# Gated norm of the state space branch: Silu(z) at its eviction, one product per row, one pair of ones matmuls, the norm's weight in the split

## What is computed

```python
z_ssm, xbc, dt_raw, q, k, v, z_att, f_logit, g_logit = jnp.split(proj, offsets, axis=-1)
y_ssm = _ssd_branch(z_ssm, xbc, dt_raw, ...)
...
def _rmsnorm(x, w):
    y = xf * lax.rsqrt(jnp.mean(xf * xf, axis=-1, keepdims=True) + EPS)
    return (y * w.astype(jnp.float32)).astype(x.dtype)
...
    # end of _ssd_branch
    return _rmsnorm(y * jax.nn.silu(z), ssm_norm_w)
...
merged = g_ssm * jnp.einsum("bse,ed->bsd", y_ssm, w_proj_ssm) + ...
```

## Time and profile before

| what | value |
|---|---|
| timed executions, median | 2098.41 us (2098.94, 2098.41, 2094.1) |
| profiled execution, its own time | 2096.4 us |
| its span in the trace | 2094.9 us |
| what lies around the span | 1.5 us |
| mean granted clock of TensorE | 0.973 of full speed |
| TensorE busy | 1967.2 us (94%) |
| stage 2 in the trace | about 209 to 445 us |
| stage 3 | about 445 to 510 us |
| stage 4 | from 510 us |

### The profile page before, as it was taken

One profiled execution on the slowest core, in us unless ns is written; L12 is line 12 of the kernel. 1 busy time (PEld: TensorE's weight loads), 2 busy tenths in 40 slices (PEclk: granted clock), 3 DMA queues, 4 the chain that ended last, 5 costly groups with the idle time before them and its releaser, 6 DMA issues. The chain is left out here.

```text
span 2094.9 us, 26015 instructions
## 1 busy us (share of the span) xinstructions
PE 1967.2 (94%) x9712; PEld 1580.1 (75%) x9712; DVE 997.0 (48%) x1217; ACT 756.3 (36%) x1136; POOL 167.2 (8%) x311
## 2 busy tenths in 40 slices
PE   6899999998999999999999999879999998999897
PEld 3678778776787887888878788657777776787786
DVE  4576544555422334333343344488333335554865
ACT  4423233234213443444433342242343434422422
POOL 0000110000010000000000000012100002101100
PEclk8899999999999999999999999999999999999999
DMA  7441665533431111111111443423201111111302
GB/s 284 170 72 41 101 112 99 111 111 120 140 103 39 41 40 50 30 40 40 40 50 40 141 131 101 140 58 89 88 21 43 33 30 60 43 48 28 129 28 90
DMA packets 165319, 166.35 MB, mean 79 GB/s; under 512 B 11402, under 2 KB 143938, under 8 KB 163970
## 3 DMA queue, kind: packets, MB, share of 16 engines
q1 hardware_dynamic: 151746, 116.11, 18.0%
q0 software_dynamic: 13504, 49.29, 10.3%
HBM read 132.22 MB, written 33.16 MB: 79 GB/s over the span
## 5 line engine op out<-in xcount | busy, mean ns | idle before, releaser
L288 PE MATMUL acc<-ha_hi,w_hi 128*128 128x512 f32 x1152 | 471.6, 409 | 11.5 <-ACT nxt L301 7.2
L288 PE MATMUL acc<-ha_hi,w_lo 128*128 128x512 f32 x1152 | 453.0, 393 | 0.0
L288 PE MATMUL acc<-ha_lo,w_hi 128*128 128x512 f32 x1152 | 452.1, 392 | 0.0
L288 PEld LDWEIGHTS acc<-ha_hi,w_hi 128*128 128x128 f32 x1152 | 218.7, 190 | 57.4 <-issue 11.6
L288 PEld LDWEIGHTS acc<-ha_hi,w_lo 128*128 128x128 f32 x1152 | 218.0, 189 | 48.4
L288 PEld LDWEIGHTS acc<-ha_lo,w_hi 128*128 128x128 f32 x1152 | 218.9, 190 | 42.1
L257 DVE TENSOR_TENSOR w_lo<-w_raw,w_hi 128x1024 fp32r<-128x1024 f32 x128 | 157.5, 1230 | 140.2 <-ACT w_hi L253 137.2
L271 PE MATMUL acc<-ha_hi,w_hi 128*128 128x512 f32 x592 | 188.0, 399 | 27.9 <-DVE ha_lo L1740 13.7
L271 PE MATMUL acc<-ha_lo,w_hi 128*128 128x512 f32 x592 | 185.0, 394 | 0.0
L271 PE MATMUL acc<-ha_hi,w_lo 128*128 128x512 f32 x592 | 184.8, 394 | 0.0
L271 PEld LDWEIGHTS acc<-ha_hi,w_hi 128*128 128x128 f32 x592 | 111.1, 191 | 58.7 <-issue 15.8
(11 more groups left out here) (437 smaller groups left out, 2777.1 us busy)
## 6 DMA issues: line engine op xcount, KB each, us to landing
w_raw<-in_w_in SPq DMA_DIRECT2D x99, 512.0 KB, 3.9
w_ada<-in_w_ada SPq DMA_DIRECT2D x8, 1024.0 KB, 11.8
acs_bc<-acs_scr POOLq DMA_DIRECT2D x8, 1024.0 KB, 15.9
w_raw<-in_w_out SPq DMA_DIRECT2D x11, 512.0 KB, 3.9
x_tok<-in_x SPq DMA_DIRECT2D x8, 512.0 KB, 6.5
xt_scr<-xt SPq DMA_DIRECT2D x1, 4096.0 KB, 22.6
w_ada_g<-in_w_ada SPq DMA_DIRECT2D x8, 512.0 KB, 9.7
z_scr<-stash SPq DMA_DIRECT2D x8, 512.0 KB, 10.8
```

The lines of the kernel that those rows point to most:

```text
L288: mm = pe.matmul(acc[:, 0, half * HALF:(half + 1) * HALF], w[:, n % 2, k, :], x[:, k, half * HALF:(half + 1) * HALF], start=(k == 0 and i ...
```

## The change

- `read_half` takes a function, and the z tiles of stage 2 are read from PSUM with Silu in place of Copy. z_scr then holds silu(z), and stage 3 has no Silu.
- Stage 3 forms one product per row, xbc = xbc * silu_z. ya_hi is Copy(xbc) with the norm's weight as a scale per partition; ya_lo is xbc * weight - ya_hi in one VectorE operation. Squares go to y_sq, a buffer of two rows, in the place of yw.
- VectorE adds all 8 squared rows into xbc row 0 (7 additions in place of 4), and the ones matmuls read that row alone (2 in place of 8).
- On VectorE the product of row f + 1 stands ahead of the low part of row f. The order of the gate reads and the weight splits on ScalarE and VectorE is another, and the split of tile 31 (N_MIX1) has a place of its own.

```diff
@@ -291,14 +291,14 @@
...
-        def read_half(act, n, half, m, dst, adv=0):
+        def read_half(act, n, half, m, dst, adv=0, func=ACT.Copy):
 
             if half:
                 projected(act, n, adv=adv)
             else:
                 act.wait_ge(half_done, m + 1)
             s = slice(half * HALF, (half + 1) * HALF)
-            return act.activation(dst[:, s], acc[:, 0, s], ACT.Copy).then_inc(fill_free, 1)
+            return act.activation(dst[:, s], acc[:, 0, s], func).then_inc(fill_free, 1)
 
...
@@ -971,7 +971,7 @@
             def read_tile(c, i):
                 act.wait_ge(stash_saved[i], 16 * c + 16)
                 for half in range(2):
-                    read_half(act, N_Z + 2 * c + i, half, 2 * c + i, stash[:, i, :])
+                    read_half(act, N_Z + 2 * c + i, half, 2 * c + i, stash[:, i, :], func=ACT.Copy if i else ACT.Silu)
                 act.drain().then_inc(stash_ready[i], 1)
 
...
@@ -1078,8 +1078,8 @@
         silu_z = Region(at_arena + XBC_TILES * T * 4, arena_end)("silu_z", [P, 2, T])
-        yw = Region(at_arena + 8 * T * 4, arena_end)("yw", [P, 2, T])
-        z_loaded, z_silued = [sem("z_loaded0"), sem("z_loaded1")], sem("z_silued")
+        y_sq = Region(at_arena + 8 * T * 4, arena_end)("y_sq", [P, 2, T])
+        z_loaded, sq_added = [sem("z_loaded0"), sem("z_loaded1")], sem("sq_added")
...
@@ -1121,67 +1121,78 @@
         def act_3(act):
             begin_stage(act, 3)
             act.drain().then_inc(ga_saved, 16)
-            for j in range(2):
-
-                def silu(b):
-                    f = 4 * j + b
-                    act.wait_ge(z_loaded[b % 2], 16 * (f // 2) + 16)
-                    act.activation(silu_z[:, b % 2, :], silu_z[:, b % 2, :], ACT.Silu).then_inc(z_silued, 1)
-
-                def tile(b):
-
-                    act.wait_ge(yz_done, 4 * j + b + 3)
-                    act.activation(xbc[:, 4 * j + b, :], xbc[:, 4 * j + b, :], ACT.Square).then_inc(Norm.squared, 1)
-                    act.activation(ya_hi[:, 4 * j + b, :], yw[:, b % 2, :], ACT.Copy).then_inc(x_hi_done, 1)
-
-                def gate(i, half):
-                    n = N_GATT + 2 * j + i
-                    projected(act, n)
-                    act.wait_ge(ga_saved, 64 * j + 32 * i + 16 * half + 16)
-                    e = act.activation(ga_half[:, :], acc[:, n % 2, half * HALF:(half + 1) * HALF], ACT.Copy)
-                    if half:
-                        e.then_inc(acc_free[n % 2], 1)
-                    act.drain().then_inc(ga_ready, 1)
-
-                if j:
-                    split_hi(act, N_GATT + 3)
-                silu(0)
-                silu(1)
-                tile(0)
-                silu(2)
-                tile(1)
-                gate(0, 0)
-                split_hi(act, N_GATT + 2 + 2 * j)
-                silu(3)
-                tile(2)
-                gate(0, 1)
-                tile(3)
-                gate(1, 0)
-                gate(1, 1)
+
+            def tile(f):
+                act.wait_ge(yz_done, f + 3)
+                act.activation(ya_hi[:, f, :], xbc[:, f, :], ACT.Copy, scale=dcol(vec1, VEC1, "ssm_norm_w", f)).then_inc(x_hi_done, 1)
+                if f >= 2:
+                    act.wait_ge(sq_added, f - 1)
+                act.activation(y_sq[:, f % 2, :], xbc[:, f, :], ACT.Square).then_inc(Norm.squared, 1)
+
+            def gate(i, half):
+                n = N_GATT + i
+                projected(act, n)
+                act.wait_ge(ga_saved, 32 * i + 16 * half + 16)
+                e = act.activation(ga_half[:, :], acc[:, n % 2, half * HALF:(half + 1) * HALF], ACT.Copy)
+                if half:
+                    e.then_inc(acc_free[n % 2], 1)
+                act.drain().then_inc(ga_ready, 1)
+
+            for f in range(3):
+                tile(f)
+            gate(0, 0)
+            split_hi(act, N_GATT + 2)
+            tile(3)
+            gate(0, 1)
+            tile(4)
+            tile(5)
+            gate(1, 0)
+            split_hi(act, N_GATT + 3)
+            tile(6)
+            gate(1, 1)
+            tile(7)
+            gate(2, 0)
+            split_hi(act, N_MIX1)
+            gate(2, 1)
+            gate(3, 0)
             split_hi(act, N_MIX1 + 1)
+            gate(3, 1)
             end_stage(act, 3)
 
         def dve_3(dve):
             begin_stage(dve, 3)
             dve.drain().then_inc(yz_done, 2)
-            for f in range(KT):
-                b = f % 2
-                if f and b == 0:
-                    split_lo(dve, N_GATT + f // 2 + 1)
-                dve.wait_ge(z_silued, f + 1)
-                dve.scalar_tensor_tensor(yw[:, b, :], xbc[:, f, :], dcol(vec1, VEC1, "ssm_norm_w", f), silu_z[:, b, :],
-                                         ALU.mult, ALU.mult)
-                dve.tensor_tensor(xbc[:, f, :], xbc[:, f, :], silu_z[:, b, :], ALU.mult)
+
+            def gated(f):
+                dve.wait_ge(z_loaded[f % 2], 16 * (f // 2) + 16)
+                dve.tensor_tensor(xbc[:, f, :], xbc[:, f, :], silu_z[:, f % 2, :], ALU.mult)
                 dve.drain().then_inc(yz_done, 1)
+
+            def low(f):
                 dve.wait_ge(x_hi_done, SPLITS[3] + f + 1)
                 if f == 6:
                     for i in range(2):
                         dve.wait_ge(stash_saved[i], 16 * (NCHUNK + 1))
-                dve.tensor_tensor(ya_lo[:, f, :], yw[:, b, :], ya_hi[:, f, :].bitcast(F32), ALU.subtract
-                                  ).then_inc(x_lo_done, 1)
-                if b:
-                    dve.wait_ge(Norm.squared, f + 1)
-                    dve.tensor_tensor(xbc[:, f - 1, :], xbc[:, f - 1, :], xbc[:, f, :], ALU.add)
+                dve.scalar_tensor_tensor(ya_lo[:, f, :], xbc[:, f, :], dcol(vec1, VEC1, "ssm_norm_w", f),
+                                         ya_hi[:, f, :].bitcast(F32), ALU.mult, ALU.subtract).then_inc(x_lo_done, 1)
+
+            def add_square(f):
+                dve.wait_ge(Norm.squared, f + 1)
+                dve.drain()
+                a = y_sq[:, 0, :] if f == 1 else xbc[:, 0, :]
+                dve.tensor_tensor(xbc[:, 0, :], a, y_sq[:, f % 2, :], ALU.add).then_inc(sq_added, 2 if f == 1 else 1)
+
+            gated(0)
+            for f in range(KT):
+                if f in (4, 7):
+                    split_lo(dve, N_GATT + (2 if f == 4 else 3))
+                if f + 1 < KT:
+                    gated(f + 1)
+                low(f)
+                if f >= 2:
+                    add_square(f - 1)
+            add_square(KT - 1)
+            split_lo(dve, N_MIX1)
             split_lo(dve, N_MIX1 + 1)
             end_stage(dve, 3)
 
@@ -1205,11 +1216,9 @@
 
         def pe_4(pe):
             begin_stage(pe, 4)
-            for f in range(0, KT, 2):
-                for h in range(2):
-                    mm = pe.matmul(work[:, h, :], ones[:, :], xbc[:, f, h * HALF:(h + 1) * HALF],
-                                   start=(f == 0), stop=(f == KT - 2))
-                mm.then_inc(norm4.summed, 2)
+            for h in range(2):
+                mm = pe.matmul(work[:, h, :], ones[:, :], xbc[:, 0, h * HALF:(h + 1) * HALF], start=True, stop=True)
+            mm.then_inc(norm4.summed, KT)
...
```

## The result

The changed kernel takes 2086.57 us as the median of 12 runs (2080.98 to 2090.94), against 2098.27 us for the kernel before in 12 runs (2091.43 to 2103.1). The ratio is 0.9938, with a 95% interval of 0.9924 to 0.9952: 0.5 to 0.8% faster, some 10 to 16 us. By the medians that is 11.7 us; the prediction's sum was 11.6 and its forecast 2085.4. The profiled execution took 2086.67 us, with a span of 2085.2 us.

What follows compares the result with a forecast made beforehand. TensorE was taken as the bound, 94% busy, held in stage 3 by the row-by-row exchange between ScalarE and VectorE. Terms of -6.0, -2.3, -4.9, +1.3 and +0.3 sum to -11.6 us: 2085.4 from 2097.0, range 2080.5 to 2092.

Steps and rivals of the forecast that it cites:

- The wait ahead of tile 31: Stage 3: TensorE's idle stretch before tile 31, laid to a late gate read on ScalarE, goes whole: -6.0 us.
- The walk of stage 3: Operation-by-operation timing of stage 3's new lists: w_lo of tile 30 ready at 477.4, needed at 479.9, the tightest place.
- rival B: Stage 3 is late at another place: w_lo of tile 30 2 us too late, +4.2 us, 2089.6; chance 0.12.
- The clock behind it: Tile 31, behind the removed wait, runs at full clock in place of partly 1.2 GHz: -2.3 us.
- The ones matmuls: Between tile 31 and tile 32: two of eight remain, -4.9 us, and the gain passes through.
- Stage 2: Table loads for Silu reads cost TensorE 1.3 us at c = 0 plus 0.3 us of clock; later turns covered.
- Rival C: Stage 2 table loads not covered: every turn pays on TensorE's path, 19.4 us, net +6.2, 2103.2; chance 0.05.
- Rival D: Tile 31 waits as before, behind read, store and weight split; only the ones matmuls pay, 2093.7; chance 0.12.
- The sum: All terms over the kernel: -6.0 - 2.3 - 4.9 + 1.3 + 0.3 = -11.6 us.

Runs made afterwards that it cites:

- gate order alone: Kernel before with one line moved: second read of tile 29 ahead of row 6 in stage 3's second turn; 2098.98 us, ratio 1.0011 to before.
- Silu alone: Kernel before with z read out of PSUM with Silu in stage 2 and no Silu in stage 3; 2103.27 us, ratio 1.0022 to before.
- first trace of before: Unchanged kernel, its first profiled execution: 2096.4 us; stages 2 to 4 took 321.4 us, what lies behind tile 33's start 1564.1 us.
- second trace of before: Unchanged kernel, executed and traced once more: 2097.75 us; stages 2 to 4 took 319.4 us, what lies behind tile 33's start 1570.2 us.
- four more loads a turn: Changed kernel with six one-column Silu and Exp activations ahead of the Exps of each stage 2 turn but the first; 2110.78 us, ratio 1.0053 to before.

## Why the prediction was right

- **The wait ahead of tile 31** (6.0 us): gone whole, 6.0 measured. The cause was told too simply. The late gate read was the last link, but to move it alone gave nothing (gate order alone), nor did Silu alone: row 7's ya_lo and the stage's end stood right behind. What frees TensorE is the rest of the change together with the order; its parts, the shorter row and VectorE's order, were not run apart.
- **The walk of stage 3.** Counted from tile 27's start, w_lo of tile 30 was to be ready at 31.9 us and came at 32.8; the slack was 1.55 us and not 2.5. The new Copy with the weight as its scale takes 1.15 us for 1.04, the upper bound, and VectorE's wait for z row 2 was 1.69 us, not the 2.8 I wrote down. Its longest wait isn't in the prediction's text at all: 2.73 us for row 3's ya_hi (460.19, above), which stands on ScalarE behind row 2's square, a gate read and a split. The direction of the error is that of rival B, its size 0.9 of the 2.5 us from which on TensorE would have idled.
- **The clock behind it** (2.3 us): 2.3 measured.
- **The ones matmuls** (4.9 us): 5.1 measured alone in the timeline; the gain passed through to tile 33, whose wait grew by 0.35.
- **Stage 2** (1.3 + 0.3 us): the wait at c = 0 grew by 1.40, and against the first trace of before the clock took nothing more. The sum 1.6 stood for 1.4. Against the second trace of before, where the clock had not fallen behind the wait at c = 0, stage 2 lost 3.0 us. The loads of the other turns were covered with about 3.5 us left, as forecast.
- **Rival C** (loads not covered) would have needed what four more loads a turn did. The Trainium skill ("ScalarE: Activation LUTs", "Table sets: the hidden batching unit") says to batch activation calls by table set. The change goes against it, and ScalarE was 12 us more busy by the profile (756.3 to 768.4); TensorE was hurt at the first turn alone. The drain of about 1.38 us that the Trainium skill ("ScalarE: Activation LUTs", "What ACT_TABLE_LOAD costs") adds to each load does not show in the loads of the first two turns, above: each takes 1.29 us from its start to the next operation's.
- **Rival D** (tile 31 waits as before): its long chain of store, loads and split ended 7 us early, as walked.
- **Behind tile 33** the sum said nothing, and a single pair of traces would have misled: the first traces of before and changed differ by 9.7 us in span and by 11.7 in stages 2 to 4. The second trace of before lies on the other side of the changed kernel's, so this is spread as far as can be seen, not a cost.
- **The sum** (-11.6 us): stages 2 to 4 gave 11.7 against the first trace of before and 9.7 against the second, and the timed runs some 10 to 16. That sum and medians agree to 0.1 us is luck, with terms off by 0.2 to 0.35 us both ways and a single trace to start from; that they agree to some 2 us is not.

## What to carry to other kernels

A wait that has one visible last link may have others right behind it: before a move is made, look at what comes next on every engine, and measure the parts alone, since here neither moving the read nor taking Silu out gave anything by itself. In this kernel an operation that costs ScalarE a table switch was free as long as the tile it serves was wanted later than the switch ended, so read that slack from the trace at every place, the first turn of a loop above all, where nothing has been prepared. And when such a gap closes, the next transfer that was hidden behind it is due earlier: expect a new wait one turn on.

## What the runs showed that was not expected

The same instructions behind tile 33 took between 1563.0 and 1572.8 us in the twelve traces that have the same code there, and the granted clock is where it shows. A stretch of 200 us from the second block, in the first trace of before and, 5 us earlier as that trace is, in the second:

```profile
1750.00:1950.00 200.00, 181.91 (x1003) 149.04 (x1004) 110.99 (x166) 80.58 (x130) 35.98 (x62) 0.96 0.20 61
```

```profile
1745.00:1945.00 200.00, 182.63 (x990) 150.03 (x991) 106.64 (x162) 76.28 (x126) 35.42 (x58) 0.94 0.17 52
```

0.02 of 200 us is 4 us. Ahead of stage 2, too, the traces differ: its first transpose comes at 206.4 to 207.4 us in nine of them and at 209.4 to 210.0 in five, and the kernel before is in either group. Of the waits of 2.2 to 3 us that TensorE made in stages 2 to 4, some had the fall to 1.2 GHz behind them and others of the same length in another execution had not. Why one and not the other is open. For the reader it means that one trace tells most waits of a place to 0.1 us (the one ahead of tile 31 in the kernel before to 0.4: 5.86 and 5.49), and a whole span to no better than some 5 us.
